# Delta rule's triangular inverse: the first four doublings in 32-row blocks on 32x32 array tiles, the fifth as a join

## What is computed

```python
    lower = jnp.where(strict, jnp.einsum("bhnid,bhnjd->bhnij", kb, k) * decay, 0.0)
    rhs = jnp.concatenate([vb, kb * jnp.exp(g)[..., None]], axis=-1)
    sol = lax.linalg.triangular_solve(lower, rhs, left_side=True, lower=True, unit_diagonal=True)
    u, w = sol[..., :dv], sol[..., dv:]
```

## Time and profile before

| | before |
|---|---|
| device time, median of 3 runs | 1241.87 us (1240.96 to 1243.59) |
| profiled execution, first to last instruction (span) | 1238.9 us |
| mean granted clock of TensorE, share of full | 0.999 |
| TensorE matmul busy | 1221.6 us (99%), 6615 records |
| TensorE weight loads busy | 994.8 us (80%) |
| VectorE busy | 688.8 us (56%) |
| ScalarE busy | 625.6 us (50%) |
| GpSimd busy | 65.1 us (5%) |
| weights and activations read from HBM | 145.31 MB |

### The profile page before, as it was taken

How to read it: one execution, slowest core, us unless ns; L and a number is a source line. 1 busy time by engine, 2 the same in 40 slices (tenths; PEclk the granted TensorE clock), 3 DMA queues, 4 the chain that set the end, 5 groups by cost and what they waited for, 6 DMA issues and landing times.

```text
span 1238.9 us, 18199 instructions
## 1 busy us (share of the span) xinstructions
PE 1221.6 (99%) x6615; PEld 994.8 (80%) x6615; DVE 688.8 (56%) x998; ACT 625.6 (50%) x1145; POOL 65.1 (5%) x96
## 2 busy tenths in 40 slices
PE   7999999999999999999999999999999999999998
PEld 5788888888888787777788888878888888888887
DVE  4567667675665794887684565566733333332221
ACT  4577677776554666666854344443532233231221
POOL 0000000001110000000221210003000000000000
PEclk9999999999999999999999999999999999999999
DMA  9777776796663332212221123653233333343320
GB/s 326 208 204 197 199 185 177 185 234 162 162 154 103 84 95 77 69 51 69 69 86 53 57 65 102 187 153 97 74 102 102 94 92 102 100 119 104 111 85 26
DMA packets 278055, 152.41 MB, mean 123 GB/s; under 512 B 8021, under 2 KB 273390, under 8 KB 277998
## 3 DMA queue, kind: packets, MB, share of 16 engines
q1 hardware_dynamic: 273626, 149.49, 43.7%
q10 hardware_dynamic: 4372, 2.15, 0.6%
HBM read 145.31 MB, written 6.29 MB: 122 GB/s over the span
## 4 chain that ended last, share of the span: by engine, by line
PE 91%; ACT 3%; DVE 2%; DMA 2%; issue 1%; SPq 1%; ACTq 0%; DVEq 0%
PE region L1709 12%; PE region L1713 12%; PE region L1718 12%; PE tail L1709 9%; PE tail L1713 8%; PE tail L1718 8%; PE tail L1699 5%; PE tail L1701 5%; PE tail L1700 5%; DMA gates<-kept_gates 1%; PE region L1699 1%; DMA ada_early<-in_w_ada 1%; PE region L2169 1%; PE region L2161 1%; PE region L1701 1%
## 5 line engine op out<-in xcount | busy, mean ns | idle before, releaser
L605 ACT ACTIVATE w_hi<-raw 128x1024 fp32r<-128x1024 f32 (+1 forms) x177 | 197.3, 1114 | 403.8 <-PE region L1718 204.7
L1101 DVE TENSOR_TENSOR w_lo<-raw,w_hi 128x1024 fp32r<-128x1024 f32 (+1 forms) x176 | 229.3, 1303 | 201.1 <-ACT w_hi L605 200.1
L1709 PE MATMUL region<-u_hi,w_hi 128*128 128x512 f32 x640 | 158.4, 390 | 0.1
L1718 PE MATMUL region<-u_hi,w_lo 128*128 128x512 f32 x640 | 158.1, 389 | 0.0
L1713 PE MATMUL region<-u_lo,w_hi 128*128 128x512 f32 x640 | 158.1, 389 | 0.0
L1709 PEld LDWEIGHTS region<-u_hi,w_hi 128*128 128x128 f32 x640 | 119.9, 188 | 25.9 <-issue 0.8
L1718 PEld LDWEIGHTS region<-u_hi,w_lo 128*128 128x128 f32 x640 | 120.1, 188 | 25.0
L1713 PEld LDWEIGHTS region<-u_lo,w_hi 128*128 128x128 f32 x640 | 120.1, 188 | 24.9
L625 ACT ACTIVATE ada_raw<-ada_raw,cond 128x128 f32<-128x128 f32 x448 | 134.2, 388 | 0.9 <-DMA ada_raw<-in_w_ada 0.8
L1699 PE MATMUL tail<-u_hi,w_hi 128*128 128x512 f32 x264 | 107.7, 408 | 0.3 <-DVE w_lo L1101 0.3
L1701 PE MATMUL tail<-u_hi,w_lo 128*128 128x512 f32 x264 | 103.2, 391 | 0.0
(11 more groups left out here) (375 smaller groups left out, 1639.3 us busy)
## 6 DMA issues: line engine op xcount, KB each, us to landing
raw<-in_w_ffn_in SPq DMA_DIRECT2D x168, 256.0 KB, 3.4
ada_raw<-in_w_ada SPq DMA_DIRECT2D x56, 512.0 KB, 5.1
raw<-in_w_in SPq DMA_DIRECT2D x90, 256.0 KB, 3.3
raw<-in_w_ffn_out SPq DMA_DIRECT2D x32, 384.0 KB, 5.3
raw<-in_w_ffn_out SPq DMA_DIRECT2D x32, 320.0 KB, 4.3
ada_early<-in_w_ada SPq DMA_DIRECT2D x8, 1024.0 KB, 10.9
gates<-kept_gates SPq DMA_DIRECT2D x16, 256.0 KB, 4.1
raw<-in_w_out SPq DMA_DIRECT2D x16, 256.0 KB, 3.2
```

The costliest lines, as they stand in the source:

```text
L605: act.activation(w_hi[:, slot % 2, 0:k, :], raw[:, slot, 0:k, :], ACT.Copy).then_inc(hi_ready, 1)
L1101: dve.tensor_tensor(w_lo[:, slot % 2, 0:k, :], raw[:, slot, 0:k, :], w_hi[:, slot % 2, 0:k, :].bitcast(f32), ALU.subtract).then_inc(lo_rea ...
L1709: pe.matmul(bank(b), w_hi[:, slot, n, :], x_hi[:, x0 + n, :], start=start and n == 0, stop=False)
L1718: ins = pe.matmul(bank(b), w_lo[:, slot, n, :], x_hi[:, x0 + n, :], start=False, stop=stop and n == k - 1)
```

## The change

The first four doublings run in the four 32-row diagonal blocks of each head, `part(r)` now being rows 32r to 32r+31, on four 32x32 array tiles. The transposed inverse is kept beside the inverse in `inv[..., HB:HB + QB]`. At level 4 VectorE writes the results to their places in the 64-row blocks, in seven instructions per block. The fifth doubling is a join: the entries of the system below the diagonal between neighbouring 32-row blocks (0 with 1, 2 with 3) are multiplied with the inverse of the one and then of the other, on one or two tiles at a time, and VectorE writes three negated blocks. The join of the 64-row blocks and all later steps are as before. The fill points and their sizes stay. ScalarE's copies read `tiles32(region[..][:, 0:P])`, 128x128 elements instead of 128x256. GpSimd makes six masks of 32 columns (two additions of halves instead of two copies for each), and clears `inv_t` and a part of `inv` ahead of the levels of each block; VectorE's clearing (line 1600) is gone.

```diff
-            for l in range(6):
+            then(fold(ident[:, :], 5))
+            for l in range(5):
...
+                for b in (2 * pair, 2 * pair + 1):
+                    if pair:
+                        pool.wait_ge(uw_ps, b - 1)
+                    pool.memset(inv[0:QB, b % 2, :, QB:HB], 0.0)
+                    pool.memset(inv_t[:, b % 2], 0.0).then_inc(zeroed, 1)
...
-                for l in range(2, JOIN + 1):
+                for l in range(2, JOIN):
...
-                        act.activation(blocks64(prod, b % 2), tiles64(region[b % 2][:, 0:DNH * HB]), ACT.Copy)\
+                        act.activation(blocks32(prod, b % 2), tiles32(region[b % 2][:, 0:P]), ACT.Copy)\
...
-                    for q in range(2):
-                        ins = dve.tensor_copy(link[part(q), e, :, HB:P], sys_t[part(q), e, :, part(q)])
+                    for r in range(4):
+                        ins = dve.tensor_copy(link[part(r), e, :, QB:HB], sys_t[part(r), e, :, part(r)])
...
-                        dve.tensor_tensor(inv[rows_i, e, :, 0:HB], inv[rows_i, e, :, 0:HB],
-                                          tiles64(region[e][rows_i, S:S + DNH * HB]), ALU.subtract)
+                        corr, corr_t = (tiles32(region[e][:, S + at:S + at + P]) for at in (0, S // 2))
+                        if l < JOIN - 1:
+                            dve.tensor_tensor(blocks32(inv, e), blocks32(inv, e), corr, ALU.subtract)
+                            ins = dve.tensor_tensor(blocks32(inv, e, HB), blocks32(inv, e, HB), corr_t, ALU.subtract)
+                        elif l < JOIN:
+                            dve.tensor_tensor(inv[part(1), e, :, QB:HB], inv[part(1), e, :, 0:QB], corr[part(1)],
+                                              ALU.subtract)
+                            for r in (0, 2):
+                                dve.tensor_tensor(inv[part(r), e, :, 0:QB], inv[part(r), e, :, 0:QB], corr[part(r)],
+                                                  ALU.subtract)
+                            dve.wait_ge(zeroed, b + 2)
+                            for r in range(4):
+                                ins = dve.tensor_tensor(inv_t[part(r), e, :, part(r)], inv[part(r), e, :, HB:HB + QB],
+                                                        corr_t[part(r)], ALU.subtract)
                         else:
+                            dve.tensor_scalar(inv[part(1), e, :, 0:QB], corr[part(1)], -1.0, None, ALU.mult)
+                            for r in (0, 2):
+                                ins = dve.tensor_scalar(inv_t[part(r), e, :, part(r + 1)], corr_t[part(r)], -1.0, None,
+                                                        ALU.mult)
...
-                for b in both:
-                    dve.wait_ge(inv_ready, 2 * JOIN * pair + 2 * (JOIN - 1) + b % 2 + 1)
-                    dve.memset(inv_t[HB:P, b % 2, :, 0:HB], 0.0)
...
-                for l in range(1, JOIN + 1):
+                for l in range(1, JOIN):
...
-                            for q in range(2):
-                                ins = pe.matmul(region[e][part(q), h * HB:(h + 1) * HB], link[part(q), e, h, 0:HB],
-                                                inv[part(q), e, h, 0:HB], start=True, stop=True)
+                            for r in range(4):
+                                ins = pe.matmul(region[e][part(r), h * QB:(h + 1) * QB], link[part(r), e, h, 0:QB],
+                                                inv[part(r), e, h, 0:QB], start=True, stop=True)
...
-                            for q in range(2 if l < JOIN else 1):
+                            for r in range(4 if l < JOIN - 1 else 3):
+                                pe.matmul(region[e][part(r), S + h * QB:S + (h + 1) * QB], inv[part(r), e, h, HB:HB + QB],
+                                          prod[part(r), e, h, 0:QB], start=True, stop=True)
                         for h in range(DNH):
-                            for q in range(2):
+                            for r in range(4):
+                                ins = pe.matmul(region[e][part(r), S + S // 2 + h * QB:S + S // 2 + (h + 1) * QB],
+                                                prod[part(r), e, h, 0:QB], inv[part(r), e, h, HB:HB + QB],
+                                                start=True, stop=True)
...
+                    for h in range(DNH):
+                        for r in (0, 2):
+                            ins = pe.matmul(region[e][part(r + 1), h * QB:(h + 1) * QB], sys_t[part(r), e, h, part(r + 1)],
+                                            inv[part(r), e, h, 0:QB], start=True, stop=True)
+                    ins.then_inc(prod_ps, 1)
...
+                    for h in range(DNH):
+                        pe.matmul(region[e][part(1), S + h * QB:S + (h + 1) * QB], inv_t[part(1), e, h, part(1)],
+                                  prod[part(1), e, h, 0:QB], start=True, stop=True)
+                        for r in (0, 2):
+                            ins = pe.matmul(region[e][part(r), S + S // 2 + h * QB:S + S // 2 + (h + 1) * QB],
+                                            prod[part(r + 1), e, h, 0:QB], inv_t[part(r + 1), e, h, part(r + 1)],
+                                            start=True, stop=True)
+                    ins.then_inc(corr_ps, 1)
+                fill("level")
```

More of the change, by code:

```diff
@@ L60 @@
 HB = P // 2
+QB = P // 4
 JOIN = 5
@@ L548, in _, with fold @@
             pool.wait_ge(u_lo_ready, 3 * KD)
-            pool.memset(pad[:, :, 0:TAPS - 1], 0.0).then_inc(pad_zero, 1)
+            pool.memset(pad[:, :, 0:TAPS - 1], 0.0).then_inc(zeroed, 1)
             pool.wait_ge(y_ps, SBH // 2)
             pool.wait_ge(conv_step, 48)
-            for q in range(2):
-                then(pool.tensor_copy(level[part(q), 6, :], ident[part(q), part(q)]))
-            m = sys_t[:, 1, 0, :]
-            for l in range(6):
+            m, sums = sys_t[:, 1, 0, :], sys_t[:, 1, 1, 0:HB]
+            def fold(t, l):
+                then(pool.tensor_tensor(sums, t[:, 0:HB], t[:, HB:P], ALU.add))
+                return pool.tensor_tensor(level[:, l, :], sums[:, 0:QB], sums[:, QB:HB], ALU.add)
+            then(fold(ident[:, :], 5))
+            for l in range(5):
                 k = 1 << l
@@ L2141, in _ @@
                     for h in range(DNH):
-                        for q in range(2):
-                            ins = pe.matmul(region[e][part(q), h * HB:(h + 1) * HB], inv_t[part(q), e, h, 0:HB],
-                                            level[part(q), 6, :], start=True, stop=True)
+                        for r in range(4):
+                            ins = pe.matmul(region[e][part(r), h * QB:(h + 1) * QB], inv[part(r), e, h, HB:HB + QB],
+                                            level[part(r), 5, :], start=True, stop=True)
                     ins.then_inc(inv0_ps, 1)
@@ L2177, in _ @@
                     fill("level")
+                for b in both:
+                    e = b % 2
+                    pe.wait_ge(inv_ready, 2 * JOIN * pair + 2 * (JOIN - 2) + e + 1)
+                    for h in range(DNH):
[3 more added lines that the diff above has]
+                    ins.then_inc(prod_ps, 1)
+                for b in both:
+                    e = b % 2
+                    pe.wait_ge(prod_ready, 2 * JOIN * pair + 2 * (JOIN - 1) + e + 1)
+                    for h in range(DNH):
[7 more added lines that the diff above has]
+                fill("level")
                 for b in both:
```

46 lines of the change are left out of this document (18 added, 28 removed).

## The result

The changed kernel takes 1249.1 us in the median (1246.19 to 1254.25, 4 runs) against 1241.83 (1240.96 to 1243.59, 4 runs): ratio 1.0063, 95% interval 1.0048 to 1.0077. It is slower by 7.3 us where 8.4 us less were forecast. The profiled execution took 1248.4 us with a span of 1246.7, which is 7.8 above the 1238.9 of the kernel before and 16.2 above the 1230.5 of the forecast. The mean granted clock of the four executions was 0.989 to 0.993, and the slowest of them had the lowest.

A forecast was written before the change was run, and what follows sets the result against it. TensorE's queue was taken to bound the kernel. Savings of 7.7 (levels 1 to 4), 3.6 (level 5) and 0.7 us (first transposition), 12.0 together, less 3.6 given back, net 8.4, gave 1233.5 us; range 1230 to 1249.

The forecast's parts named there:

- What bounds the kernel: Whole span: TensorE nearly always has work, matmuls 99% of the span, so a microsecond saved in a level shortens the span.
- Spacing of records on four tiles: Levels 1 to 4: records on four 32x32 tiles follow each other at 10 ns, between bounds of 6 and 31.
- The floor of 25 ns: Skill page's issue floor for matmuls of up to 64 columns; with it the kernel would be some 13 us slower.
- rival 3: TensorE's small records: one per 31 ns whatever the tile, giving 1266 us; chance 15%.
- Prod to first correction: Start of each level 1 to 4: 1.17 us becomes 0.91, saving 0.26.
- Level 5: Fifth doubling as a join: 3.18 us becomes 1.37, saving 3.6 us over two pairs.
- a wait of 1.0: Before the join's prod: TensorE waits 1.0 us for VectorE's level 4 operations, twice, 2.0 us given back.
- The step that failed: TensorE's supply: about 1,600 more instructions cost nothing beyond 2 ns in the record spacing.
- rival 2: Supply of TensorE's instructions: records come at 14 to 20 ns, giving 1239.5 us at 16 and 1246 at 20; chance 13%.
- The prediction's own sign of being wrong: Levels 1 to 4: the forecast is wrong if waits add up to more than 4 us.
- The give-backs of 1.6 us in levels 2 and 3: Where projections no longer cover VectorE and ScalarE: 0.9 us in first pair's level 2, 0.3 and 0.4 in second pair's levels.
- Net gain: Whole kernel: 12.0 us saved less 3.6 us given back, net 8.4 us.

The follow-up runs named there:

- equal places: Two projection chunks at each of three places inside levels 1 to 4: changed kernel 1241.53 us, the kernel before with the same places 1249.34 us.
- the burst: The kernel before with 512 extra 32x32 records on four tiles in the first pair, results unused: 1253.96 us.
- the kernel with transposes and two chunks: The changed kernel with VectorE transposing the corrected inverse instead of TensorE's transposed corrections, two projection chunks behind each level as before: 1237.37 us.
- five chunks: The changed kernel with five projection chunks instead of two at each level's fill point: 1241.93 us.
- four chunks: The changed kernel with four projection chunks instead of two at each level's fill point: 1244.66 us.
- two chunks at each place: The changed kernel with two projection chunks after both prods and after each block's corrections in levels 1 to 4: 1241.53 us.

## Why the prediction was wrong

**What bounds the kernel**: right. TensorE is the queue that counts, and every microsecond of its stalls is in the span.

**Spacing of records on four tiles**: right in the array, 8.5 ns for the 10 taken (bounds 6 and 31). The floor of 25 ns that the prediction set beside it did not show, and rival 3 with it. Prod to first correction 0.86 us for 0.91, the copy 0.28 for 0.29, an undisturbed level 3.75 for 3.8. Level 5 missed: the two took 4.68 and 6.29 us (666.81 to 671.49, 730.78 to 737.07) where 2.95 and a wait of 1.0 were forecast. Of the 3.1 us too much, 1.1 is VectorE's wait, 1.44 and 1.65 us for 1.0; its operations of 32x128 come 0.29 apart for the 0.24 taken; most of the rest is the second of them running at the lower clock behind that wait.

**The step that failed** is the one that reads "TensorE has about 1,600 more instructions to be supplied with; I cost that at nothing beyond the 2 ns in the spacing". The burst rate was taken for the lasting one. The supply is a bound of its own, 27 ns a record, and rival 2, which named it, was sized by a slower spacing of 14 to 20 ns, not by stops between blocks, and given 13%. The prediction's own sign of being wrong, waits of over 4 us in levels 1 to 4, came with 9.3 us. Its remark that "96 records and six others in 4.76 us is all that a long stretch ever asked for" was the right evidence: 204 instructions in 4.76 us are 23 ns each, 15 in the densest part, and nothing in the profile had shown less.

**The size.** The eight levels 1 to 4, from prod to prod, took 38.3 us before, should have taken 30.6 and took 45.7 (643.45 to 666.81, 708.43 to 730.78). Of these 15.1 us 9.3 are the six stalls; the other 5.8 are by their rows the lower clock behind them, about 1 us after each long one in the projection matmuls and the rest in the small ones. With level 5's 3.1 this is 18.2. The give-backs of 1.6 us in levels 2 and 3 did not come, since a TensorE that is late waits for nobody, which leaves 16.6, against the 16.2 us between forecast and trace.

**The clock** was no term of the forecast. The earlier trace rows show it in full, in a kernel whose TensorE hardly idled; the prediction should have asked what happens when it does.

**Net gain**: at equal places and full supply the change is worth 7.8 us, against 8.4 forecast. That the two are so near is in part luck: the levels gave more than forecast, and level 5 gave 0.95 us of its 3.6.

## What to carry to other kernels

Before cutting matmuls into smaller ones for packing, count instructions against time: in the densest 256, a weight load and a matmul being two, TensorE here gets no more than one per 13.6 ns once the block ahead is used up. If the small tiles would go faster than 27 ns a record, save instructions as well (here: let VectorE transpose what TensorE computed twice), or put long matmuls between the small ones in every 256, not behind two levels' worth. A stall marked "issue" in the midst of one line, at a fixed distance in instructions from the last, is this supply; and one of 2 us can cost another 1 us or more in granted clock behind it.

## What the runs showed of the hardware

- TensorE's instructions arrive by 256 (16.4 KB); when a block is issued in less than 3.5 us, TensorE stops until some 3.5 us after the block's start (3.47 between the starts of blocks in the burst; 3.8 in the kernel with transposes and two chunks). A stop needs no load on the DMA engines: in the burst they moved three packets in 12 us.
- 32x32 records on four tiles start 8.5 ns apart, 64x64 records on two tiles 29.6 ns apart, over 512 records.
- Each stretch of lower clock (1.2 GHz) within the levels and joins stood during or within 2.1 us behind a stop or wait of TensorE of 1.6 to 2.8 us. Not each such stop lowered it: after 1.98 and 1.89 us (five chunks), 1.55 (four chunks) and a wait of 1.81 (two chunks at each place) it stayed in full, and so it did through stops of 0.3 to 1.2 us, one every 3.7 us.
- VectorE's transpose of the 32x32 blocks of a 128x128 tile took 0.31 us, a subtraction of that size 0.27; on 32x128 the transpose took 0.30.
